# Attention in a decoder layer: value products with stationary values on two column tiles, turned back by transposes

## What is computed

```
qc = qg[block c] * scale
s = einsum('bqkgd,bnkd->bkgqn', qc, k_cmp); p_cmp = masked_softmax(s - slope*dist)      # 63 compressed keys
o_cmp = einsum('bkgqn,bnkd->bqkgd', p_cmp, v_cmp)
imp = einsum('bkgqn,nj->bkqj', p_cmp, ov)          # importance of the 16 key blocks; the top 8 are selected
o_slc = softmax over the keys of the selected blocks, times v_s
o_win = softmax over the last 256 keys, times v_w
o = gate[0]*o_cmp + gate[1]*o_slc + gate[2]*o_win
```

## Time and profile before

| | us |
|---|---|
| median of 3 runs (lowest, highest) | 1056.08 (1053.9, 1059.67) |
| the profiled execution's own time | 1058.48 |
| its span, first to last instruction | 1056.7 |
| attention, first scores to last values | 300.3 to 581.0 |
| granted TensorE clock over the span | 0.995 of full |

### The profile page before, as it was taken

How to read it: one execution, slowest core, us unless ns; L and a number is a source line. 1 busy time by engine, 2 the same in 40 slices (tenths; PEclk the granted TensorE clock), 3 DMA queues, 4 the chain that set the end, 5 groups by cost and what they waited for, 6 DMA issues and landing times.

```text
span 1056.7 us, 14288 instructions
## 1 busy us (share of the span) xinstructions
PE 1027.7 (97%) x4759; PEld 617.8 (58%) x4760; DVE 643.5 (61%) x1630; ACT 323.4 (31%) x766; POOL 175.4 (17%) x214
## 2 busy tenths in 40 slices
PE   8999999999999999999999999999989999999997
PEld 4544475444546877778779885555564444444443
DVE  3331121455454777776643898765578688877985
ACT  3321121111133766565665763332110000000000
POOL 0030051111000400000000400211021333323333
PEclk8999999999999999999999999999999999999999
DMA  7310042012000200000000504232649869999432
GB/s 262 103 45 28 1 82 79 1 40 84 20 1 1 81 2 1 1 2 2 1 1 1 200 2 133 100 120 80 238 161 367 294 234 345 338 383 340 137 113 91
DMA packets 73687, 119.23 MB, mean 113 GB/s; under 512 B 14016, under 2 KB 53152, under 8 KB 73632
## 3 DMA queue, kind: packets, MB, share of 16 engines
q1 hardware_dynamic: 62544, 87.55, 24.6%
q0 software_dynamic: 11088, 30.95, 8.3%
HBM read 105.37 MB, written 21.50 MB: 120 GB/s over the span
## 4 chain that ended last, share of the span: by engine, by line
PE 51%; DVE 12%; issue 3%; DMA 3%; ACT 2%; POOL 0%; POOLq 0%; DVEq 0%; ACTq 0%
PE ps L1804 14%; PE ps L1150 9%; PE ps L1814 7%; PE ps L2127 5%; PE ps L1118 4%; PE ps L1129 4%; PE ps L1171 3%; PE ps L2137 2%; DMA big_w<-hn_dram,misc 2%; DVE ring_gate_up L1276 1%; DVE big_w L1618 1%; PE ps L2158 1%; DVE big_u L2346 1%; ACT big_u L1226 1%; DVE misc L291 1%
## 5 line engine op out<-in xcount | busy, mean ns | idle before, releaser
L1618 DVE STREAM_TRANSPOSE big_w<-big_w 32x256 f32<-32x256 f32 x384 | 167.3, 436 | 34.7 <-DMA big_w<-hn_dram,misc 28.4
L1804 PE MATMUL ps<-ring_gate_up,big_w 128*128 (+1 forms) x400 | 179.9, 593 | 1.9 <-DVE big_w L1618 1.5
L517 PE MATMUL ps<-big_w,big_u 128*128 128x512 f32 (+1 forms) x448 | 175.8, 547 | 1.7 <-DMA big_w<-in_w_in 1.7
L517 PEld LDWEIGHTS ps<-big_w,big_u 128*128 128x128 f32 x448 | 84.2, 193 | 78.5 <-issue 71.9
L1804 PEld LDWEIGHTS ps<-ring_gate_up,big_w 128*128 128x128 f32 x400 | 73.9, 190 | 85.6 <-issue 85.6
L1150 PEld LDWEIGHTS ps<-ring_down,big_u 128*128 128x128 f32 x912 | 109.7, 192 | 15.7 <-issue 12.1
L1150 PE MATMUL ps<-ring_down,big_u 128*128 128x65 f32 x912 | 116.3, 273 | 0.5 <-DVE big_w L1303 0.4
L1226 ACT ACTIVATE big_u<-ps 128x512 f32<-128x512 f32 (+1 forms) x126 | 69.4, 582 | 112.9 <-PE ps L1129 112.7
L1276 DVE CUSTOM_DVE_ANT_0 ring_gate_up<-ps,ring_down 128x384 f32<-128x384 f32 (+7 forms) x128 | 73.8, 629 | 43.2 <-PE ps L1118 42.7
L1218 ACT ACTIVATE ring_gate_up<-ring_gate_up,big_w 128x64 f32<-128x64 f32 (+8 forms) x192 | 92.2, 555 | 1.1 <-DVE big_w L1276 1.1
L1814 PE MATMUL ps<-ring_down,big_w 128*128 x200 | 90.0, 593 | 0.6 <-ACT big_w L1848 0.6
(11 more groups left out here) (389 smaller groups left out, 1351.2 us busy)
## 6 DMA issues: line engine op xcount, KB each, us to landing
ring_gate_up<-in_w_gate SPq DMA_DIRECT2D x16, 1024.0 KB, 10.4
ring_gate_up<-in_w_up SPq DMA_DIRECT2D x16, 1024.0 KB, 13.2
ring_down<-in_w_down SPq DMA_DIRECT2D x16, 1024.0 KB, 14.8
misc<-in_x SPq DMA_DIRECT2D x16, 512.0 KB, 4.0
big_w<-in_w_in SPq DMA_DIRECT2D x6, 1024.0 KB, 7.2
big_w<-in_w_out SPq DMA_DIRECT2D x8, 512.0 KB, 5.2
hn_dram<-big_u SPq DMA_DIRECT2D x8, 512.0 KB, 2.6
out<-ring_gate_up SPq DMA_DIRECT2D x8, 512.0 KB, 3.8
```

The source lines that it names most:

```text
L517: last = nc.tensor.matmul(ps[:, b, 0:width], uT[:, k, c * P:(c + 1) * P], wbuf[:, n % 2, k, 0:width], start=(k == 0), stop=(k == KD - 1))
L1618: last = nc.vector.transpose(dst[j * 32:(j + 1) * 32, :, i * 32:(i + 1) * 32], src[i * 32:(i + 1) * 32, :, j * 32:(j + 1) * 32])
L1804: last = nc.tensor.matmul(ps[:, 2 + b, :], xT[:, b, k, :], ring_gu[:, bass.ds(at + k * 2 * D_EXP, BANK)], start=(k == 0), stop=(k == KD - 1))
```

## The change

Four things change together.

1. **values** of WIN and SEL slots: the values (128 keys x 64) are now stationary, and the transposed weights are moving, 128 columns for each head of the slot's group. The two key/value groups write partitions 0 to 63 and 64 to 127 of bank 6 (two column tiles of the array). The output has channels in rows, so it must be **turned**: ACT copies the bank to SBUF (`copy_values`), PE transposes it four times (`turn_values`), and DVE reads the turned bank. CMP slots use both groups' rows at once (`v_cmp` holds each group's values in columns of its own), 128 moving columns; the importance has products of its own into a bank of its own.
2. The denominator no longer comes from a column of ones: `exponentials` asks ACT for the row sum of each `exp` (`accum_out`), which adds one accumulator read on ACT to each of the 192.
3. Three banks (4, 5, 7) take turns for transposes, turns, importance and selection.
4. In slots of three or four banks (**wide**) all of values(j-2) stands between the second and the third bank of transposes(j-1); in others ahead of them. The group that ended in slot l is copied, turned and read in iteration l+3; ACT's copy stands ahead of copy_weights(j-1), PE's turn ahead of the transposes. A first slot of a group waits until the group before is copied (`bank_is_free`). The last group's copy stands in the SSD mixer's list on ACT.

```
+CMP_V = NG * (HD + N_BLK)
...
-    rows = np.zeros((NG, CMP_COLS, HD + 17), np.float32)
-    rows[:, 0:N_CMP, HD:] = np.concatenate([np.ones((N_CMP, 1)), ov / L_CMP], axis=1)
-    c["v_cmp_start"] = rows.reshape(P, HD + 17)
+    rows = np.zeros((NG, CMP_COLS, CMP_V), np.float32)
+    for g in range(NG):
+        rows[g, 0:N_CMP, NG * HD + g * N_BLK:NG * HD + (g + 1) * N_BLK] = ov / L_CMP
+    c["v_cmp_start"] = rows.reshape(P, CMP_V)
...
-            nc.vector.tensor_copy(M["v_cmp"][64:64 + N_CMP, 0:HD], ps[64:64 + N_CMP, 3, 0:HD]).then_inc(c_read, 1)
+            nc.vector.tensor_copy(M["v_cmp"][64:64 + N_CMP, HD:2 * HD], ps[64:64 + N_CMP, 3, 0:HD]).then_inc(c_read, 1)
...
+    o_T = M["misc"][:, 2048:3072].rearrange("p (b n) -> p b n", b=2)
+    O_BANK, TURN_BANKS = 6, (4, 5, 7)
...
+    turned = [gi for gi, (br, c) in enumerate(groups) if br != CMP]
+    turns_before = lambda gi: sum(1 for x in turned if x < gi)
+    turn_at = {last_slot[groups[gi]] + 3: gi for gi in turned}
+    imp_at = {last_slot[CMP, c] + 2: c for c in sel_count}
+    bank_users, copy_use, sel_use, imp_use, turn_use, prep_use = [], [], {}, {}, {}, None
+    for j in range(J + 3):
+        if j in imp_at:
+            imp_use[imp_at[j]] = len(bank_users)
+            bank_users.append((imp_read, sel_count[imp_at[j]]))
+        if j in turn_at:
+            while j == J + 2 and TURN_BANKS[len(bank_users) % 3] != 7:
+                bank_users.append(bank_users[-3])
+            turn_use[turn_at[j]] = len(bank_users)
+            bank_users.append((o_read, turn_at[j] + 1))
...
-            if use >= 2:
-                pe.wait_ge(*bank_users[use - 2])
-            return 4 + use % 2
+            if use >= 3:
+                pe.wait_ge(*bank_users[use - 3])
+            return bank_of(use)
...
-            blocks = banks_of(j)[k]
-            for i in range(len(blocks)):
-                at = (j % 2) * 2048 + k * BANK + i * P
+            blocks, (gi, br, c, pairs), n = banks_of(j)[k], slots[j], columns(j)
+            for i, (g, r, blk) in enumerate(blocks):
+                at = (j % 2) * 2048 + (i * P if br == CMP else ((r - pairs[0]) * NG + g) * n + blk * P)
                 last = nc.tensor.transpose(ps[:, bank, i * P:(i + 1) * P], w_rows[:, at:at + P], ident[:, :])
...
-        def values(j, a, b):
+        def bank_is_free(gi):
+
+            if groups[gi - 1][0] == CMP:
+                pe.wait_ge(o_read, gi)
+            else:
+                pe.wait_ge(oT_copied, turns_before(gi))
+
+        def compressed_values(j):
 
             gi, br, c, pairs = slots[j]
-            if a == 0:
-                if j == first_slot[br, c] and gi >= 1:
-                    pe.wait_ge(o_read, gi)
-                pe.wait_ge(wT_done, copies_before[j + 1])
-            blocks = blocks_of(j)
-            w = HD + 17 if br == CMP else HD + 1
-            for x in range(a, b):
-                g, r, blk = blocks[x]
-                if br == CMP:
-                    for g in range(NG):
-                        rows = slice(g * 64, (g + 1) * 64)
-                        last = nc.tensor.matmul(ps[:, 6 + g, r * w:(r + 1) * w], weightsT(j, 0)[rows, x * P:(x + 1) * P],
-                                                v_cmp[rows, 0:w], start=True, stop=True)
-                    continue
-                at = key_blocks(br, c)
-                last = nc.tensor.matmul(ps[:, 6 + g, r * w:(r + 1) * w], weightsT(j, x // 4)[:, (x % 4) * P:(x % 4 + 1) * P],
-                                        vals[br][:, at[blk], g, :], start=(blk == 0), stop=(blk == len(at) - 1))
-            if b == len(blocks) and b > a:
-                last.then_inc(pv_done, 1)
+            pe.wait_ge(wT_done, copies_before[j + 1])
+            rows = [weightsT(j, 0)[:, r * P:(r + 1) * P] for r in pairs]
+            if c in sel_count:
+                bank = transpose_bank(imp_use[c])
+                for r in pairs:
+                    nc.tensor.matmul(ps[:, bank, r * NG * N_BLK:(r + 1) * NG * N_BLK], rows[r], v_cmp[:, NG * HD:CMP_V],
+                                     start=True, stop=True)
+            if gi >= 1:
+                bank_is_free(gi)
+            for r in pairs:
+                last = nc.tensor.matmul(ps[:, O_BANK, r * P:(r + 1) * P], rows[r], v_cmp[:, 0:NG * HD], start=True, stop=True)
+            last.then_inc(pv_done, 1)
+
+        def values(j):
+
+            gi, br, c, pairs = slots[j]
+            if j == first_slot[br, c]:
+                bank_is_free(gi)
+            pe.wait_ge(wT_done, copies_before[j + 1])
+            blocks, m = key_blocks(br, c), len(pairs)
+            for b, blk in enumerate(blocks):
+                for g in range(NG):
+                    x = (b * NG + g) * m
+                    last = nc.tensor.matmul(ps[g * HD:(g + 1) * HD, O_BANK, pairs[0] * P:(pairs[-1] + 1) * P],
+                                            vals[br][:, blk, g, 0:HD], weightsT(j, x // 4)[:, x % 4 * P:(x % 4 + m) * P],
+                                            start=(b == 0), stop=(b == len(blocks) - 1))
+            last.then_inc(pv_done, 1)
+
+        def turn_values(gi):
+
+            pe.wait_ge(oT_copied, turns_before(gi) + 1)
+            bank = transpose_bank(turn_use[gi])
+            for r in range(GQ):
+                last = nc.tensor.transpose(ps[:, bank, r * P:(r + 1) * P], o_T[:, turns_before(gi) % 2, r * P:(r + 1) * P],
+                                           ident[:, :])
+            last.then_inc(o_turned, 1)
...
-        for j in range(J + 2):
-            n_v = len(blocks_of(j - 2)) if j >= 2 else 0
+        for j in range(J + 3):
             n_t = len(banks_of(j - 1)) if 1 <= j <= J else 0
             if j < J:
                 scores(j)
-            v = 0
-            if n_v and slots[j - 2][1] == CMP:
-                values(j - 2, 0, n_v)
-                v = n_v
+            if 2 <= j < J + 2 and slots[j - 2][1] == CMP:
+                compressed_values(j - 2)
             if j in piece_at:
                 z_pieces(piece_at[j][0], piece_at[j][1])
             if j == J + 1:
                 next_tensor(pe)
+            wide_values = 2 <= j < J + 2 and slots[j - 2][1] != CMP
+            if wide_values and n_t <= 2:
+                values(j - 2)
+            if j in turn_at:
+                turn_values(turn_at[j])
+            if j in piece_at:
+                z_pieces(piece_at[j][1], piece_at[j][2])
             for k in range(n_t):
-
-                upto = n_v if n_t <= 2 and not k else max(v, n_v * (k + 1) // (n_t + 1) if k >= 2 else (n_v + 1) // 2)
-                if v < upto:
-                    values(j - 2, v, upto)
-                    v = upto
-                if k == 0 and j in piece_at:
-                    z_pieces(piece_at[j][1], piece_at[j][2])
+                if wide_values and k == 2:
+                    values(j - 2)
                 transposes(j - 1, k)
...
-                last = nc.scalar.activation(w, w, ACT.Exp, bias=neg[:, br, h:h + 1], scale=-1.0)
+                last = nc.scalar.activation(w, w, ACT.Exp, bias=neg[:, br, h:h + 1], scale=-1.0,
+                                            accum_out=den[c % 2][:, br, h:h + 1])
             last.then_inc(exp_done, 1)
+
+        def copy_values(gi):
+            act.wait_ge(pv_done, last_slot[groups[gi]] + 1)
+            nc.scalar.activation(o_T[:, turns_before(gi) % 2, :], ps[:, O_BANK, :], ACT.Copy).then_inc(oT_copied, 1)
...
         for j in range(J + 1):
+            if j in turn_at:
+                copy_values(turn_at[j])
             if j >= 1:
                 copy_weights(j - 1)
...
-            dve.wait_ge(pv_done, last_slot[br, c] + 1)
-            w = HD + 17 if br == CMP else HD + 1
-            O = ps[:, 6:8, 0:GQ * w].rearrange("p g (r n) -> p g r n", r=GQ)
+            bank = O_BANK if br == CMP else bank_of(turn_use[gi])
+            O = ps[:, bank, :].rearrange("p (r g d) -> p g r d", r=GQ, g=NG)
             dst, tmp = by_head(o_att[:, c, :]), by_head(M["o_tmp"])
             gate_at = {CMP: 0, SEL: 1, WIN: 2}[br]
-            d, f = (v[:, br, :].rearrange("p (g r) -> p g r", g=NG) for v in (den, coef))
+            d, f = (v[:, br, :] for v in (den[c % 2], coef))
+            dve.wait_ge(exp_done, last_slot[br, c] + 1)
             if br == CMP:
-                o.done(nc.vector.tensor_scalar(d, O[:, :, :, HD], 1.0e-30, None, ALU.max))
-                o.done(nc.vector.reciprocal(d, d))
+                o.done(nc.vector.tensor_scalar(d, d, 1.0e-30, None, ALU.max))
+            o.done(nc.vector.reciprocal(d, d))
+            o.done(nc.vector.tensor_tensor(f, d, sg[:, c, :, gate_at], ALU.mult))
+            fb = f.rearrange("p (g r) -> p g r", g=NG).unsqueeze(3).broadcast_to([P, NG, GQ, HD])
+            if br == CMP:
+                dve.wait_ge(pv_done, last_slot[br, c] + 1)
+                o.done(nc.vector.tensor_tensor(dst, O, fb, ALU.mult))
+                dve.sem_inc(o_read, 1)
+                if c in sel_count:
```

(23 more changed lines are left out.)

39 lines of the change are left out of this document (19 added, 20 removed).

## The result

The changed kernel takes 1101.17 us (median of 4 runs, 1098.97 to 1101.98) where the kernel before takes 1055.17 on the same chip: 1.0425 times as long, 95% interval 1.0389 to 1.046. The forecast was slower, 1071 us, in a range up to 1112. The direction and the range held; the rise is 46 us and not 15, so one or more terms are missing or too small.

A forecast was written before the change was run, and what follows sets the result against it. PE bounds the kernel before; afterwards ACT's loop would bind attention at 234.3 us against 222.9. Adding 11.4 in the rounds, 1 before and 2.4 at the end gives +14.8, so 1071 us, range 1045 to 1112.

The forecast's parts named there:

- the loop: Attention: transposes wait for exps, exps for ACT's copies, copies for the previous slot's transposes; summed to 234.3 us.
- the 40 rounds: Attention from slot 5 to 45, each from one slot's first weight transpose to the next's: 222.9 us, forecast +11.4.
- Column tiles together: Value products: the two groups' instructions run side by side on two column tiles, 0.1075 us a pair.
- a rival with a chance of 0.20: Value products' column tiles take turns, 0.215 us a step: +33.8 us, about 1105; chance 0.20.
- Change of tile shape: PE in attention: each switch costs about 0.14 us; two more in each of 25 rounds, one in some 12: 8.7 us.
- Accumulator read: ACT, after each of 152 exps in the rounds: 0.09 us each, 13.7 us, between 0 and 33.4.
- C to W: Attention round from a CMP slot to a WIN slot: forecast to go from 3.31 to 5.4 us.
- W to W: Attention round between two WIN slots: forecast to go from some 5.6 to 4.7 us.
- S7: Attention rounds of chunk 7's SEL slots: forecast to go from 7.65 to 7.0 us.
- Before slot 5: Early attention: the gate's products fill PE and hide most of the loop's cost, +1 us (0 to 3).
- at the end: After attention: the copy of the last values delays ACT's chunk 0 of the SSD mixer; +2.4 us with the last round.
- A lower granted clock for an idler PE: PE in the rounds: a clock below the present 1.00 would add time; given no size and left out of the sum.

The follow-up runs named there:

- the other waits: Changed kernel with importance read first and ACT's group copy early, value products still behind two banks: 1068.48 us; with values ahead of all transposes too, 1034.14.
- all three edits: Changed kernel with importance read first on DVE, value products ahead of all transposes, and ACT's group copy ahead of the exponentials: 1034.14 us.
- The fillers: Changed kernel with 217 identity transposes added on PE in its idle stretches in 17 slots: 1094.75 us.
- both gone: Changed kernel with importance read first on DVE and 198 identity transposes filling PE's idle time: 1080.46 us.

## Why the prediction was right in direction and short in size

- **What bounds.** Right. "I sum the loop over the 40 rounds, as if PE always waited" holds, and so does "the value products become cheaper but move into the loop that now binds". The place costs 34.3 us in the changed form once the other waits are gone (18.6 with them), and 29.2 on the kernel before, of which 9.6 lie in two rounds with a low clock. PE's work in the rounds was forecast at 186 us: the profile has 202.6 at a clock of 0.93, and 188.9 at 0.99 with all three edits.
- **Column tiles together.** Right: 0.1075 us for a pair of instructions stands (12 of 256 columns in 1.51 us), and the run with one tile at a time shows that it hangs on their turn. The Trainium skill, "TensorE: Matmul & The Clock Gate", section "Part 3: Packing small matmuls — row/col tiling", says that matmuls on different column tiles run concurrently. The trace agrees: 32 instructions of 128 columns take 1.97 us with the tiles in turn.
- **The row against it was misread.** The prediction took the compression's 0.111 for each instruction as "the price of one after the other", and built a rival with a chance of 0.20 on it. The starts in the same trace say otherwise. These instructions start in pairs too (275.99 and 276.00, then 276.21 and 276.22), as those of the changed kernel do, but a pair takes 0.213 us for 126 columns where it takes 0.109 for 128 there. So the tiles worked side by side already, and it was the pair that took twice as long. The step of 16 is the difference that the prediction named; no run changed it, so that it is the cause is not shown.
- **Change of tile shape.** As written, the two readings of the earlier trace rows give 0.20 - 0.11 = 0.09 and nothing more, since 7 x 0.056 + 0.27 is 0.66. The 0.14 is right all the same. In that trace the eight scores start in pairs, the second pair 0.16 behind the first and the later ones 0.11 apart, which is the missing 0.05, and in the changed kernel the same two steps are 0.20 (from 603.34 to 603.54) and 0.16.
- **Accumulator read.** Right: 0.095 for 0.09, 16.1 us in all for 13.7.
- **Rounds by kind.** Undisturbed rounds fit: C to W 5.64 for 5.4, W to W 4.75 for 4.7, S7 7.00 for 7.0. Before slot 5 +1.7 for +1; at the end +1.2 for +2.4.
- **Where it failed, first.** "DVE has 150.0 us for 234 and stays off the path" and "The third bank removes a wait of 0.2 that the sum has left out already." The share of DVE is right and says nothing of its order. The importance products got a bank of the same three, and its release was put behind two group reads on DVE. The sum has no term for it: 12.7 us of waits and, with the lower clock behind three of them, 15.2 us in four rounds, 14.2 of the kernel's time.
- **Where it failed, second.** "A lower granted clock for an idler PE ... would add to the time and is not in the sum." It was named and given no price. It came: 0.93 in the rounds. The fillers gave 6.4 us of the kernel's time back, 6.9 in five rounds; the 2.5 in the four rounds above come on top. The waits of PE for ACT's copy at a turn, in or behind which it fell in the other rounds, are in the sum's own terms.
- **The rest.** With both gone the rounds take 239.3 for 234.3 and the kernel 1080.5 for 1071. Of these 9.5 us, 5.0 are in the rounds (2.8 of them in those of slots 6 to 8), and 1.8 before them, which start at 350.05 and so 2.8 later than before, where the forecast had 1. The last 2.7 are a matter of counting: the forecast took 2.4 off for the profiled execution, and this run's is 0.3 under its median. What delays slots 6 to 8 and the start beyond the forecast was not tested. The profiled rise is 40.5 and that of the medians 46.0, since the two profiled executions lie 3.3 above and 2.2 below their medians.
